# Moving the SBUF addresses of all split-product operands to one residue: 128 modulo 256 bytes

## The chip, the cores and the metric

The kernel is one program on one core of a Trainium2 chip. The metric is device time in microseconds (us), the median of several runs. A profile is one execution taken by the hardware profiler. Engines: TensorE (PE for matmuls, PEld for its weight loads), VectorE (DVE), ScalarE (ACT), GpSimd (POOL) and SyncE (SP, which here issues most DMAs).

## The reference

A sequence of 512 tokens with width 1024 runs through three blocks, all in float32:

```python
# block 1, layer 0: state-space mixer (SSD), then a convolutional FFN (width 2816)
# block 1, layer 1: conformer convolution (31 taps), then the same kind of FFN
h = h + mixer(rms_norm(h, norm_mix[i]))
h = h + (silu(gt) * val) @ down_w      # gt, val = split(causal_dwconv(rms_norm(h) @ up_w))
# block 2: hybrid mixer (latent attention + S5 scan + gates), memory cross attention,
x = layer_norm(ALPHA * x + mix); x = layer_norm(ALPHA * x + xattn(x, mem))
# then a mixture of 64 experts, top 8, expert width 256, plus a shared expert
x = layer_norm(ALPHA * x + moe(x))
```

## The kernel before

**Split products.** Most matrix products are made from three passes. An operand w is split into a high part (a copy of w rounded to the type fp32r, made by ScalarE) and a low part (w minus the high part, made by VectorE). The product is hi·hi + hi·lo + lo·hi, each pass a matmul with 512 moving columns of fp32r, accumulated in PSUM. I call three such matmuls a triple. In `proj_split` (the matmul is line 1289) it reads:

```python
for q, (wp, xp) in enumerate(((0, 0), (0, 1), (1, 0))):
    ins = nc.tensor.matmul(b[:], parts[wp][:, kk, m * P:(m + 1) * P], xparts[xp][:, kk, :],
                           start=n_k == 0 and q == 0, stop=n_k == k - 1 and q == 2)
```

The first operand is the stationary one (128 columns, loaded by LDWEIGHTS while the matmul before it streams), the second the moving one. The same triple stands in `project` (lines 1396 to 1398, the SSD input projection, four banks in turn), `proj_halves` (1313), `proj_abreast` (1337, the conformer's input projection, two banks in turn), the FFN's first slot (1545 to 1547), the conformer's taps (1590 to 1592, with diagonal weights and a moving operand that shifts by 4 bytes from tap to tap), the query projection (1815 to 1817), and the experts (1983 to 1985 gate and up, 2005 to 2007 down; there the tokens are stationary and the weights move). Other products, such as line 1245 and 1800, are plain float32 matmuls.

**Buffers.** Long-lived buffers are declared one after the other: `ident`, `ones`, `tri`, `stri`, `kc` (four constants), `pcol` (parameters as columns), `hT`, `uT`, `sq` (each 8 x 512 floats), two weight slots `wring`, four row buffers `raw` of 515 floats, `std`, `rinv`, and a large `arena`. The stages carve their own buffers out of the arena with `carve` and `carve_r`, by a running offset `top`. Each declaration is rounded up to 32 bytes. `ident` begins at byte 16512 of each partition, which is 128 modulo 256. The 16 bytes of `kc` (rounded to 32) shift all that follows, and the `raw` rows (2060 bytes, rounded to 2080) shift `std`, `rinv` and the arena.

**Where the operands begin**, modulo 256 bytes, worked out from the declarations (a slice of a weight or activation buffer begins at a multiple of 512 bytes inside it, so the residue of the buffer is that of its slices):

| operands | stage | before | after |
| --- | --- | --- | --- |
| `hT`, `uT`, `sq`, `wring` and their fp32r views | all | 160 | 128 |
| arena, whole multiples of 64 floats inside it (`yhi`, `ff_lo`, `gm`, `xe_hi`, `xe_lo`, `wdn`, `act_hi`) | several | 32 | 128 |
| `whi`, `ffhi`: high parts at the arena's end | FFN, mixers | 224 | 128 |
| `wgu_hi[0]`, `wdn_hi`: high parts of expert weights | experts | 180 | 128 |
| `dghi`, `dglo`: diagonal weights of taps | conformer | 224 | 128 |
| `hghi`, `hglo`: moving rows of taps | conformer | 224 and 88, plus 4 per tap | 128, plus 4 per tap |

So one triple's pairs of moving and stationary residues are: lines 1396 to 1398, all 160; L1289 on `sq_r`, `uT_r`, L1337 and L1313, moving 160, stationary 224 (high weights) and 160 (low weights); the FFN's down projection, moving 224 and 32, stationary 160; the SSD output projection, moving 32, stationary 224 and 160; the experts, moving 160 and 160 or 180 and 160, stationary 32 (down: moving 180 and 32, stationary 32).

**The order of work.** TensorE runs through the stages in program order: SSD (to about 340 us), its output projection (to 500), FFN 0 (to 860), conformer (to 1080), FFN 1 (to 1465), hybrid mixer and cross attention (to about 2080), experts (to about 2720), final sums. SP loads weight slots ahead, each when the matmuls that read the slot's last contents are done. In the experts' loop `m_step` SP loads 3 MB per expert into a ring of four, ScalarE and VectorE split them, and POOL gathers tokens and scatters results by indirect DMA.

Of the kernel before, what the change touches and what calls it, by code (L numbers as in the profile page):

```python
# [32 lines left out]
P = 128  # L33
T = 512
D = 1024
NK = D // P
TC = T // P
NSLOT = 2
NBANK = 4
SLOT = 8 * 512  # L40
PAD = 3
# [50 lines left out]
def cols(ap, i, n):  # L92

    return ap[:, i:i + n] if isinstance(i, int) else ap[:, bass.ds(i, n)]
# [55 lines left out]
def build(nc, A, out):  # L150

    ctx = ExitStack()
    with ctx:
        def sb(name, shape, dt=F32):
            return ctx.enter_context(nc.sbuf_tensor(name, shape, dt))

        def sb2(name, shape):

            with nc.sbuf_tensor(name + "_r", shape, F32R) as r:
                pass  # L160
            return sb(name, shape), r
# [27 lines left out]
        ones = sb("ones", [P, P])  # L189
        tri = sb("tri", [P, P])  # L190
        stri = sb("stri", [P, P])
        kc = sb("kc", [P, 4])
        pcol = sb("pcol", [P, NPB * P])
        hT, hT_r = sb2("hT", [P, NK, T])
        uT, uT_r = sb2("uT", [P, NK, T])
        sq, sq_r = sb2("sq", [P, NK, T])
        wring, wlo = zip(*[sb2(f"wring{r}", [P, SLOT]) for r in range(NSLOT)])
        raw = [sb(f"raw{r}", [P, PAD + T]) for r in range(NBANK)]
        std = sb("std", [P, T])
        rinv = sb("rinv", [P, T])  # L200
        ARENA = 28080
        arena, arena_r = sb2("arena", [P, ARENA])

        top = [0]

        def carve(*shape, dt=F32, at_=None):

            n = int(np.prod(shape))
            if dt == BF16:
                n = (n + 1) // 2  # L210
            a = top[0]
            top[0] += n
            assert top[0] <= ARENA, (top[0], ARENA)
            ap = arena[:, a:a + n]
            if dt != F32:
                ap = ap.bitcast(dt)
            if len(shape) == 2:
                ap = ap.rearrange("p (a b) -> p a b", b=shape[1])
            elif len(shape) == 3:
                ap = ap.rearrange("p (a b c) -> p a b c", b=shape[1], c=shape[2])  # L220
            return ap

        def carve_r(*shape):

            a = top[0]
            ap = carve(*shape)
            r = arena_r[:, a:top[0]]
            return ap, r if len(shape) == 1 else r.rearrange("p (a b) -> p a b", b=shape[1])

        def pcols(name, i, n=1):  # L230
            return cols(pcol, par.base[name] + i, n)
# [35 lines left out]


        pk = carve(NPB, P)
        xtok = carve(TC, D)  # L270

        top[0] = 0
# [29 lines left out]

        top[0] = ARENA - NSLOT * SLOT

# [15 lines left out]
        first_whi = carve_r(max(len(ks) for ks in FFN_EARLY), P)  # L320
        top[0] = ARENA - FFN_TILES * T
        ffhi = carve_r(FFN_TILES, T)
# [2 lines left out]

        top[0] = NBANK * T
        hg = carve(NK, T + CONF_TAPS - 1)
        glu_a = [carve(T) for _ in range(2)]
        glu_b = [carve(T) for _ in range(2)]
        cv = carve(NK, T)  # L330
        xc = sq
        HGW = T + CONF_TAPS - 1
        lnsq = arena[:, NBANK * T:NBANK * T + NK * T].rearrange("p (a b) -> p a b", b=T)
        top[0] += NK * T
        cvb = [carve(T) for _ in range(2)]
        hghi = [carve_r(HGW) for _ in range(2)]
        top[0] -= 2 * HGW + 2 * T + NK * T
        DIAGS = 10
        dghi, dglo = [list(d) for d in zip(*[(carve_r(P), carve_r(P)) for _ in range(DIAGS)])]
        hglo = [carve_r(HGW) for _ in range(2)]  # L340
        tapc_hi = carve_r(CONF_TAPS * NK)
        tapc_lo = carve(CONF_TAPS * NK)
        assert top[0] <= ARENA - NSLOT * SLOT
        PE_TAPS = [11] * (NK - 1) + [16]
# [10 lines left out]
        mag8 = carve(16, CHUNKS)  # L355
        sc_consts = carve(CONST_COLS)
        cos8 = carve(16, CHUNKS)
        GATE_TOP = 17924
        assert top[0] <= GATE_TOP
        top[0] = GATE_TOP  # L360
        posi = carve(T, dt=I32)
# [3 lines left out]
        wkr = carve(NK, 64)  # L365
        top[0] = ARENA - NSLOT * SLOT - 16 * CHUNKS
        sin8 = carve(16, CHUNKS)
# [84 lines left out]
        memk = carve(2, D)  # L452
        assert top[0] <= GATE_TOP
        top[0] -= 2 * D
        memc, mT_lo = carve_r(NK, 256)
        top[0] = GATE_TOP
        memq, mT_hi = carve_r(NK, 256)
# [46 lines left out]
        rsw = [carve(2) for _ in range(RING)]  # L504
        swt = [r[:, 1:2] for r in rsw]
        sidf = carve(1)
        slotrow = carve(P)
        slotcol = carve(2)
        posm = carve(TC, NE)
        rinfo = carve_r(TC * NE, 6)[1]  # L510
        cntf = carve(1)
        cnti = carve(1, dt=I32)
        moe_top = top[0]
        wgu_hi = (carve_r(SLOT)[1], flat(hT_r))
        wdn_hi = [carve_r(2 * D)[1] for _ in range(2)]
        top[0] = moe_top
# [3318 lines left out]
```

## Time and profile before

| | |
| --- | --- |
| median of 3 runs | 2789.91 us (2785.39 to 2795.55) |
| span of the profiled execution, first to last instruction | 2782.8 us |
| the profiled execution's own device time | not given beside its span |
| TensorE (PE) busy | 2680.2 us, 96% |
| weight loads (PEld) | 2057.9 us, 74% |
| VectorE, ScalarE, GpSimd busy | 72%, 50%, 9% |
| HBM | 165 GB/s over the span |

A matmul's busy time in the records (some 395 ns for 512 columns) overlaps that of the next one: its end is modelled. How fast matmuls follow each other is read from their starts in the timeline. A stretch in which PE is "busy" can therefore still contain slack of some nanoseconds for each matmul.

### The profile page before, as it was taken

What the parts mean: (1) busy time and instruction counts of PE and PEld (TensorE: products, weight loads), DVE (VectorE), ACT (ScalarE), POOL (GpSimd) and SP (SyncE); (2) the same over time, 40 slices, a digit from 0 to 9 for tenths busy, and PEclk for the clock granted to TensorE, in tenths of its full rate; (3) what the DMA queues carried; (4) which work ended last, traced back from release to release, by engine and by line L of the source; (5) the groups of instructions that cost most, each with busy time, mean ns of one, the idle gap of its engine ahead of it and who ended that gap; (6) DMA issues with size and microseconds to landing.
All of it is one profiled execution on the core that took longest, in us unless ns stands there. A gap on an engine that the chain in (4) does not pass through costs nothing.

```text
span 2782.8 us, 36214 instructions
## 1 busy us (share of the span) xinstructions
PE 2680.2 (96%) x12549; PEld 2057.9 (74%) x12549; DVE 1992.0 (72%) x3046; ACT 1397.4 (50%) x2137; POOL 240.5 (9%) x209
## 2 busy tenths in 40 slices
PE   8999999999999999999999989999899999999996
PEld 7877877788887877888876756676557777777772
DVE  4788744777727976778538546465559999999996
ACT  4767552222325545222324333444448887787782
POOL 0000000000000000000004400000013332212210
PEclk9999999999999999999999999999999999999998
DMA  3222212233232131233333561323449999999996
GB/s 112 72 61 68 91 61 95 88 101 103 69 104 91 61 35 61 91 103 99 83 95 122 135 124 54 107 70 120 161 173 359 358 359 361 359 352 352 349 340 255
DMA packets 258832, 435.11 MB, mean 156 GB/s; under 512 B 44315, under 2 KB 197987, under 8 KB 233891
## 3 DMA queue, kind: packets, MB, share of 16 engines
q1 hardware_dynamic: 240931, 395.61, 42.7%
q0 software_dynamic: 17792, 38.06, 4.5%
q8 instruction: 67, 1.10, 0.2%
q14 instruction: 42, 0.34, 0.0%
HBM read 416.33 MB, written 42.43 MB: 165 GB/s over the span
## 4 chain that ended last, share of the span: by engine, by line
PE 74%; DMA 12%; DVE 8%; ACT 3%; issue 2%; SPq 1%; DVEq 0%; ACTq 0%
PE tp L1289 40%; DMA wring<-in_w_exp_gu 10%; PE tp L1245 4%; PE tp L1983 2%; PE tp L1984 2%; PE tp L1985 2%; PE tp L1337 2%; PE tp L1396 2%; PE tp L1398 1%; PE tp L1397 1%; DVE wring_r L3676 1%; PE tp L1800 1%; DMA wring<-ytab 1%; PE mp L1591 1%; PE mp L1590 1%
## 5 line engine op out<-in xcount | busy, mean ns | idle before, releaser
L1289 PE MATMUL tp<-sq_r,arena_r 128*128 128x512 f32 x1056 | 417.1, 395 | 3.5 <-DVE uT_r L2820 3.5
L1289 PE MATMUL tp<-uT_r,arena_r 128*128 128x512 f32 x1056 | 417.9, 396 | 0.0
L1289 PE MATMUL tp<-sq_r,wring_r 128*128 128x512 f32 x1056 | 417.3, 395 | 0.0
L1289 PEld LDWEIGHTS tp<-sq_r,arena_r 128*128 128x128 f32 x1056 | 198.3, 188 | 55.9 <-issue 5.8
L1289 PEld LDWEIGHTS tp<-uT_r,arena_r 128*128 128x128 f32 x1056 | 198.3, 188 | 48.4 <-issue 1.4
L1289 PEld LDWEIGHTS tp<-sq_r,wring_r 128*128 128x128 f32 x1056 | 198.4, 188 | 44.0
L2792 DVE TENSOR_TENSOR wring_r<-wring,arena_r 128x2048 fp32r<-128x2048 f32 x82 | 187.1, 2322 | 56.6 <-ACT arena_r L2111 56.4
L1289 PE MATMUL tp<-arena_r,wring_r 128*128 128x512 f32 x564 | 223.7, 397 | 0.0
L2359 ACT ACTIVATE arena<-arena 128x512 f32<-128x512 f32 x44 | 27.8, 633 | 296.6 <-DVE arena L2878 296.5
L2111 ACT ACTIVATE arena_r<-wring 128x2048 fp32r<-128x2048 f32 x82 | 152.4, 1905 | 43.9 <-DMA wring<-in_b_pw_w 11.9
L3682 DVE TENSOR_TENSOR arena_r<-arena,arena_r 128x1024 fp32r<-128x1024 f32 x128 | 150.4, 1216 | 0.5 <-ACT arena_r L2705 0.5
L2878 DVE SCALAR_TENSOR_TENSOR arena<-raw,pcol,arena 128x512 f32<-128x512 f32 x176 | 132.3, 752 | 20.7 <-DVE arena L2878 4.9
L2098 ACT ACTIVATE raw<-tp 128x512 f32<-128x512 f32 x78 | 45.6, 599 | 200.7 <-PE tp L1289 133.9
L1168 POOL DMA_INDIRECT ytab<-arena x64 | 99.0, 1547 | 437.0 <-ACT arena L2724 430.7
L1289 PE MATMUL tp<-arena_r,sq_r 128*128 128x512 f32 x436 | 136.2, 393 | 0.0
L1289 PE MATMUL tp<-arena_r,uT_r 128*128 128x512 f32 x436 | 136.2, 393 | 0.0
L1396 PE MATMUL tp<-sq_r,wring_r 128*128 128x512 f32 x320 | 129.8, 406 | 0.9 <-DVE wring_r L2928 0.9
L2705 ACT ACTIVATE arena_r<-arena 128x1024 fp32r<-128x1024 f32 x128 | 127.8, 1051 | 0.0
L1398 PE MATMUL tp<-sq_r,wring_r 128*128 128x512 f32 x320 | 126.1, 394 | 0.0
L1397 PE MATMUL tp<-uT_r,wring_r 128*128 128x512 f32 x320 | 126.1, 394 | 0.0
L1289 PEld LDWEIGHTS tp<-arena_r,wring_r 128*128 128x128 f32 x564 | 105.7, 187 | 25.6
L2874 DVE TENSOR_TENSOR raw<-tp,rinv 128x512 f32<-128x512 f32 x88 | 60.5, 687 | 70.0 <-PE tp L1289 69.5
(582 smaller groups left out, 6209.2 us busy)
## 6 DMA issues: line engine op xcount, KB each, us to landing
arena<-in_w_exp_down SPq DMA_DIRECT2D x64, 1024.0 KB, 28.4
wring<-in_w_exp_gu SPq DMA_DIRECT2D x64, 1024.0 KB, 10.4
uT<-in_w_exp_gu SPq DMA_DIRECT2D x32, 1024.0 KB, 9.4
sq<-in_w_exp_gu SPq DMA_DIRECT2D x32, 1024.0 KB, 11.1
wring<-in_f_up_w SPq DMA_DIRECT2D x22, 1024.0 KB, 5.2
wring<-in_f_up_w SPq DMA_DIRECT2D x44, 512.0 KB, 6.6
wring<-in_f_down_w SPq DMA_DIRECT2D x32, 448.0 KB, 5.6
wring<-in_a_in_proj SPq DMA_DIRECT2D x42, 256.0 KB, 2.8
```

The lines of the kernel that those rows point to most:

```text
L1168: G.indirect_dma_start(out=ytab, out_offset=bass.IndirectOffsetOnAxis(ap=ridx[q][0:CAP, :], axis=0), in_=ye[b][0:CAP, :], in_offset=None, ...
L1245: ins = nc.tensor.matmul(b[lo:hi, 0:n], w, x, start=k == 0, stop=k == len(mms) - 1)
L1289: ins = nc.tensor.matmul(b[:], parts[wp][:, kk, m * P:(m + 1) * P], xparts[xp][:, kk, :], start=n_k == 0 and q == 0, stop=n_k == k - 1 and ...
L1396: nc.tensor.matmul(bank[:], w_hi[:, kk, cs], u_hi[1][:, kk, :], start=kk == 0, stop=False)
L1397: nc.tensor.matmul(bank[:], w_hi[:, kk, cs], u_lo[1][:, kk, :], start=False, stop=False)
L1398: ins = nc.tensor.matmul(bank[:], w_lo[:, kk, cs], u_hi[1][:, kk, :], start=False, stop=kk == NK - 1)
L2111: nc.scalar.activation(hi[r][1][:, a:b], wring[r][:, a:b], ACT.Copy).then_inc(whi_ready, 1)
L2705: nc.scalar.activation(wdn_hi[b][:, s], wdn[q][:, s], ACT.Copy).then_inc(moe["dhi"], 1)
L2792: V.tensor_tensor(wlo[r][:, a:b], wring[r][:, a:b], hi[r][1][:, a:b].bitcast(F32), ALU.subtract).then_inc(wlo_ready, 1)
L2874: V.tensor_tensor(r[:, PAD:PAD + T], tp[tiles.s % NBANK][:], rinv[:], ALU.mult).then_inc(tile_evac, 1)
L2878: ins = V.scalar_tensor_tensor(dst, r[:, PAD - t:PAD - t + T], w(taps - 1 - t), dst, ALU.mult, ALU.add)
L3682: V.tensor_tensor(wdn_lo[q][:, s], wdn[q][:, s], wdn_hi[b][:, s].bitcast(F32), ALU.subtract).then_inc(moe["dlo"], 1)
```

## The change

All operands of split products are given the residue 128 modulo 256 bytes. `kc` and the `raw` rows move into one tensor `tail` behind the arena, so that all large buffers follow `stri` without an odd size between. The arena grows by 16 floats. Odd sizes inside it are rounded up to 64 floats (`align`, `HGA`), and the experts' high parts are carved from the arena's end and no longer from `moe_top`. `slotrow` moves from the arena into a dead part of `pcol`. No instruction is added or taken away; four `raw` rows now begin at 2060-byte steps.

```diff
-        kc = sb("kc", [P, 4])
         pcol = sb("pcol", [P, NPB * P])
...
-        raw = [sb(f"raw{r}", [P, PAD + T]) for r in range(NBANK)]
         std = sb("std", [P, T])
         rinv = sb("rinv", [P, T])
-        ARENA = 28080
+        ARENA = 28096
         arena, arena_r = sb2("arena", [P, ARENA])
+        tail = sb("tail", [P, NBANK * (PAD + T) + 4])
+        raw = [tail[:, r * (PAD + T):(r + 1) * (PAD + T)] for r in range(NBANK)]
+        kc = tail[:, NBANK * (PAD + T):NBANK * (PAD + T) + 4]
...
+        LINE = 64
+
+        def align():
+
+            top[0] = -(-top[0] // LINE) * LINE
...
         hg = carve(NK, T + CONF_TAPS - 1)
+        align()
...
-        hghi = [carve_r(HGW) for _ in range(2)]
-        top[0] -= 2 * HGW + 2 * T + NK * T
+        HGA = -(-HGW // LINE) * LINE
+        hghi = [carve_r(HGA) for _ in range(2)]
+        top[0] -= 2 * HGA + 2 * T + NK * T
...
-        hglo = [carve_r(HGW) for _ in range(2)]
+        hglo = [carve_r(HGA) for _ in range(2)]
+        hghi, hglo = [[(f[:, 0:HGW], r[:, 0:HGW]) for f, r in h] for h in (hghi, hglo)]
...
-        GATE_TOP = 17924
+        GATE_TOP = 17920
...
-        slotrow = carve(P)
+        slotrow = pcols("a_conv_w", 0, P)
...
         moe_top = top[0]
+        assert moe_top <= ARENA - 2 * SLOT
+        top[0] = ARENA - 2 * SLOT
         wgu_hi = (carve_r(SLOT)[1], flat(hT_r))
         wdn_hi = [carve_r(2 * D)[1] for _ in range(2)]
         top[0] = moe_top
```

## Rows read from the trace of the kernel before

**Rows 1.** The page: busy time of each engine, and the chain that ended last.

```profile
PE 2680.2 (96%) x12549; PEld 2057.9 (74%) x12549; DVE 1992.0 (72%) x3046; ACT 1397.4 (50%) x2137; POOL 240.5 (9%) x209
...
PE 74%; DMA 12%; DVE 8%; ACT 3%; issue 2%; SPq 1%; DVEq 0%; ACTq 0%
```

**Rows 2.** Windows: stretch, length, busy (count) by engine, PEclk, DMA share, GB/s.

```profile
500.00:740.00 240.00, 240.00 (x1031) 193.02 (x1030) 186.75 (x231) 65.83 (x68) 0.00 (x0) 1.00 0.29 90
...
2300.00:2600.00 300.00, 288.09 (x1444) 223.76 (x1443) 283.42 (x432) 235.72 (x348) 65.88 (x58) 1.00 0.96 355
```

**Rows 3.** The page's costliest groups, four of split products: count, busy, mean.

```profile
L1289 PE MATMUL tp<-sq_r,arena_r 128*128 128x512 f32 x1056 | 417.1, 395 | 3.5 <-DVE uT_r L2820 3.5
...
L1289 PE MATMUL tp<-arena_r,wring_r 128*128 128x512 f32 x564 | 223.7, 397 | 0.0
...
L1289 PE MATMUL tp<-arena_r,sq_r 128*128 128x512 f32 x436 | 136.2, 393 | 0.0
...
L1398 PE MATMUL tp<-sq_r,wring_r 128*128 128x512 f32 x320 | 126.1, 394 | 0.0
```

**Rows 4.** Timeline, PE, SSD input projection: start, length, instruction; 13 matmuls between.

```profile
301.70 0.39 PE L1396 MATMUL tp<-sq_r,wring_r 128*128 128x512 f32 x1
...
304.88 0.39 PE L1398 MATMUL tp<-sq_r,wring_r 128*128 128x512 f32 x1
```

**Rows 5.** Timeline, PE, FFN 0 up and hybrid input projections; 23 matmuls between, each time.

```profile
560.04 0.40 PE L1289 MATMUL tp<-uT_r,arena_r 128*128 128x512 f32 x1
...
565.64 0.40 PE L1289 MATMUL tp<-uT_r,arena_r 128*128 128x512 f32 x1
...
1605.27 0.40 PE L1289 MATMUL tp<-sq_r,arena_r 128*128 128x512 f32 x1
...
1610.87 0.40 PE L1289 MATMUL tp<-sq_r,arena_r 128*128 128x512 f32 x1
```

**Rows 6.** Timeline, PE, conformer input projection; 47 matmuls between.

```profile
867.58 0.39 PE L1337 MATMUL tp<-sq_r,arena_r 128*128 128x512 f32 x1
...
878.67 0.39 PE L1337 MATMUL tp<-sq_r,arena_r 128*128 128x512 f32 x1
```

**Rows 7.** Timeline, PE, FFN 0 down projection; 26 matmuls between.

```profile
799.76 0.40 PE L1289 MATMUL tp<-arena_r,wring_r 128*128 128x512 f32 x1
...
806.00 0.40 PE L1289 MATMUL tp<-arena_r,wring_r 128*128 128x512 f32 x1
```

**Rows 8.** Timeline, PE, conformer taps: a whole triple from each of two channels.

```profile
888.38 0.39 PE L1590 MATMUL mp<-arena_r 128*128 128x512 f32 x1
...
889.07 0.40 PE L1590 MATMUL mp<-arena_r 128*128 128x512 f32 x1
...
914.23 0.40 PE L1590 MATMUL mp<-arena_r 128*128 128x512 f32 x1
...
914.93 0.40 PE L1289 MATMUL tp<-sq_r,arena_r 128*128 128x512 f32 x1
```

**Rows 9.** Timeline, PE, one expert: 17, then 11 matmuls between.

```profile
2400.76 0.39 PE L1983 MATMUL tp<-hT_r,arena_r 128*112 128x512 f32 x1
...
2404.93 0.40 PE L2005 MATMUL mp<-arena_r 128*112 128x512 f32 x1
...
2407.75 0.93 PE L1972 MATMUL tp<-ident,arena 112*128 112x112 f32 x8
```

**Rows 10.** The chain in order of time: a plain float32 product, start and length.

```profile
1905.41 13.73 PE tp L1800 x32
```

**Rows 11.** Waits, 2300 to 2600 us: who waited for whom, us, times, longest.

```profile
ACT arena_r L2698 <- DMA uT<-in_w_exp_gu: 17.2, 8, 2.4
...
PE mp L1993 <- DVE std L3688: 11.8, 27, 0.9
```

**Rows 12.** Two lines' own instructions: duration min/median/max in ns.

```profile
L2878 DVE SCALAR_TENSOR_TENSOR arena<-raw,pcol,arena x176: 750/752/755, 495.1 to 1339.1; 128x512 f32<-128x512 f32 x176
...
L3676 DVE TENSOR_TENSOR uT_r<-uT,arena_r x64: 1212/1219/1226, 2065.8 to 2679.9; 128x1024 fp32r<-128x1024 f32 x64
```

## The prediction

> **What bounds the kernel now.** I read the page first. TensorE is busy for 96% of the span and holds 74% of the chain that ended last; DMA holds 12%, VectorE 8% [rows 1]. The windows say where that holds. In FFN 0's up projection PE is busy for all 240 us at the full granted clock (1.00), VectorE for 187 us and the DMA engines for a share of 0.29: only TensorE can set the pace there. In the experts' loop three things are near their limit at once: PE 288 of 300 us, VectorE 283 us, and a DMA share of 0.96 at 355 GB/s [rows 2].
>
> "Busy" is not the whole story, because a matmul's record (395 ns) reaches over the next one. I therefore read the starts in the timeline, over stretches without a gap, and divide. This is the view on which the prediction rests:
>
> - SSD input projection, all residues 160: 301.70 to 304.88 us for 14 matmuls, 227.1 ns each [rows 4].
> - FFN 0 up, moving 160, stationary 224 and 160: 5.60 us for 24, 233.3 ns; hybrid input projection, the same residues: 5.60 us for 24, 233.3 ns [rows 5].
> - Conformer input projection, the same residues: 11.09 us for 48, 231.0 ns [rows 6].
> - FFN 0 down, moving 224 and 32, stationary 160: 6.24 us for 27, 231.1 ns [rows 7].
> - One expert, moving 160, stationary 32: 4.17 us for 18, 231.7 ns; its down product, moving 180 and 32, stationary 32: 2.82 us for 12, 235.0 ns [rows 9].
>
> The stage in which moving and stationary operands share a residue is the fastest by 4 to 8 ns a matmul. The order of the loops is a poor explanation: the conformer's projection also changes banks from triple to triple, runs the same three passes from the same `sq_r` and `uT_r`, and takes 231.0 ns, not 227.1. What differs beside the place of the high weights (residue 224 against 160) is hard to find. Residues alone do not fix the number, though: FFN 0 and the conformer have the same ones and differ by 2.3 ns. A plain float32 product is no witness: L1800 takes 13.73 us for 32 records, 429 ns each [rows 10], which is close to twice 512 columns at 2.4 GHz, and here moving and stationary lie at 160 too.
>
> **The change part by part.** It adds and removes no instruction. Its terms are these.
>
> 1. Triples before the experts, outside SSD and taps. The groups give 3 x 1056 + 564 + 2 x 436 = 4604 matmuls [rows 3] (the other two of the 1056 and the other 436 are the remaining passes of the same triples); by the program's loops the other split products of 512 columns are 772. Together 5376. Of these FFN 0's window holds 1031 [rows 2], and the hybrid input projection is six slots of 96, so 576: some 1,600 at 233.3 ns. The other 3,776 I take at 231.0. If all come to 227.1, the first lose 6.2 ns each, 9.9 us, and the rest 3.9 ns, 14.7 us. Sum 24.6 us. PE's weight loads do not stand in the way: PEld is busy 193 of 240 us in FFN 0 [rows 2]. VectorE has 53 us free in that window, some 22%, and the stage shrinks by 2.7%, so nothing new becomes late.
> 2. SSD's 3 x 320 matmuls [rows 3] have equal residues already; they keep them. Zero.
> 3. The conformer's taps, 279 matmuls. The moving operand shifts by 4 bytes from tap to tap, so it cannot keep a residue. Two triples read 0.69 us (moving 224) and 0.70 us (moving 128, stationary 224) [rows 8]. They range within about 5 ns of what they have, both ways, which is 1.4 us for 279. I take zero.
> 4. The experts: 64 times 36 matmuls, 2304. At 227.1 an expert would save 18 x 4.6 (24 x 4.6 for the whole gate and up product) and 12 x 7.9 ns, thus 110 + 95 = 0.2 us, 13 us in all. But the DMA engines are full there, and ScalarE waits for an expert's weights, 17.2 us in 8 waits for one of four such buffers, while PE waits 11.8 us in 27 short ones [rows 11]. A faster PE hands SP its buffers earlier, and the load only queues longer. Bounds: 0 and 13 us. I take 1, since DMA sets the pace and only the start of the loop and small holes in the share of 0.96 can give anything.
> 5. The S5 and attention parts run between short dependences. Some of term 1's matmuls there may be hidden; I take 1 us off.
> 6. `raw` rows now begin at 2060-byte steps, so their starts differ modulo 16. The convolution L2878 already reads `raw` shifted by one and two floats: all 176 take 750 to 755 ns. And L3676 reads `uT` at residue 160 and the high part at 180 in 1212 to 1226 ns [rows 12]. VectorE does not notice. Zero. `slotrow` in `pcol` is written once and read as before: zero; even 1% on VectorE's work in the experts, some 6 us, is hidden while DMA leads, and would be the bound if that cover went.
> 7. The weights' DMA destinations move from 160 or 32 to 128 modulo 256, multiples of 32 bytes before and after; four loads and four stores on `raw` rows at the end of the program are no longer so. The window's 355 GB/s [rows 2] comes from a mix of both old residues. Zero, with 0.3% of the experts' 600 us, 2 us, as its bound either way.
>
> Sum: 24.6 + 1 - 1 = about 25 us. The profiled execution spans 2782.8 us, 7 us under the median of 2789.9; its own device time is not given, so I take the difference from the median: **2765 us**.
>
> The Trainium skill speaks against this change. "SBUF — State Buffer", section "Who interferes with whom", gives TensorE two read ports, one for the moving operand and one for weight loads, independent of each other and of every engine. By that rule residues could not matter and the sum would be zero instead of 25 us. The trace has 227.1 against 231.0 and 233.3 ns [rows 4 to 6], which the rule leaves without a cause.
>
> **The rivals.**
>
> *No change.* The interval depends on something that goes with the SSD stage and not on residues: that it takes its two weight parts from the two `wring` slots rather than from the arena, or other engines' traffic. For: FFN 0 and the conformer differ at equal residues [rows 5, 6]. Against: the down projection has all its weights in `sq` and `wring`, stationary residue 160, and still takes 231.1 [rows 7]. Time 2790. It is what the skill's rule on the ports would give.
>
> *The experts give too.* If TensorE, busy 288 of 300 us, is the pacemaker and the DMA share of 0.96 has room, term 4 pays 13 us: 2753.
>
> *Aligned starts give more.* Every big buffer now begins on a multiple of 64 bytes; the old residues 160, 224 and 32 are all 32 modulo 64. The triples of the trace are 681 (3 x 227.1), 693 and 700 ns: they lie on steps of about 6.7 ns. If a start on a multiple saves one more step for each matmul, 5376 + 960 of them give 42 us more: 2765 - 42 = 2723. Against: the tap at moving residue 128 shows no such saving, 0.70 us a triple [rows 8]. "TensorE: Matmul & The Clock Gate", section "Wait — 56ns, not 53.3ns?" of the Trainium skill, has 215.7 ns between starts at 512 bf16 columns on a warm array; no row of this kernel comes near it.
>
> *A slower residue.* Equal residues alone are not enough: the tap whose moving and stationary operands lie at 224 takes 0.69 us a triple, 230 ns a matmul, and the only triple with a moving operand at 128 takes 0.70 us, 233.3 ns [rows 8]. Should 128 itself be a poor residue, all triples go to 234: SSD's 960 lose 6.9 ns each (6.6 us), the 1,600 lose 0.7 (1.1 us), the 3,776 lose 3.0 (11.3 us): +19 us, 2809. It decides the sign where the new mean passes about 231 ns over the 6,336 matmuls.
>
> **How the numbers follow.** Equal residues at 227, only before the experts: 0.47, with a range of its own of 2758 to 2773. No change: 0.18. Experts give too: 0.10. Aligned starts give more: 0.10. Slower residue: 0.15. What a measurement of this kernel can tell from no change is 0.3%, 8.4 us. Faster by more than that: 0.47 + 0.10 + 0.10 = 0.67; same 0.18; slower 0.15. The range leaves out the far side of the aligned case and most of the slower one: 2743 to 2797.
>
> **What would show it.** In the changed profile, 24 matmuls of FFN 0's up projection should span 5.45 us, not 5.60; the conformer's 48 should span 10.9; SSD's 14 stay at 3.18. The experts' loop should start some 24 us earlier and last as long as before, at 355 to 360 GB/s. L2878 stays at 752 ns. The prediction is wrong if intervals at 128 differ from those that SSD has at 160, or if the experts' loop changes its length by more than 3 us.

## The result, and the profile after

| | before | after |
| --- | --- | --- |
| median, 4 runs each on one chip | 2788.90 us (2785.39 to 2795.55) | 2753.56 us (2752.41 to 2756.62) |
| ratio, with its 95% interval | | 0.9879 (0.9864 to 0.9894) |
| span of the profiled execution | 2782.8 us | 2750.7 us |
| device time of that execution | not given | 2752.41 us |

The changed kernel takes 30 to 38 us less, 35 by the medians. Lines after the declarations have moved down by 12: L1289 is now L1301, L1337 is L1349, L1396 to 1398 are L1408 to 1410, L1983 and L2005 are L1995 and L2017, L2878 and L3676 are L2890 and L3688.

The page of the changed kernel, its span, its busy times and its chain, answers to [rows 1]:

```profile
span 2750.7 us, 36214 instructions
...
PE 2646.7 (96%) x12549; PEld 2054.1 (75%) x12549; DVE 1989.9 (72%) x3046; ACT 1398.5 (51%) x2137; POOL 232.0 (8%) x209
...
PE 72%; DMA 10%; DVE 10%; issue 3%; ACT 3%; DVEq 0%; SPq 0%; ACTq 0%
```

TensorE's share of the span is 96% before and after, and it still holds most of the chain. To see what became faster, read the starts again. Timeline of TensorE in the changed kernel, columns as in [rows 4]; SSD, FFN 0 up, FFN 0 down, conformer:

```profile
300.06 0.39 PE L1408 MATMUL tp<-sq_r,wring_r 128*128 128x512 f32 x1
...
303.23 0.39 PE L1410 MATMUL tp<-sq_r,wring_r 128*128 128x512 f32 x1
...
559.87 0.39 PE L1301 MATMUL tp<-sq_r,arena_r 128*128 128x512 f32 x1
...
565.31 0.39 PE L1301 MATMUL tp<-sq_r,arena_r 128*128 128x512 f32 x1
...
790.17 0.39 PE L1301 MATMUL tp<-arena_r,wring_r 128*128 128x512 f32 x1
...
796.29 0.39 PE L1301 MATMUL tp<-arena_r,wring_r 128*128 128x512 f32 x1
...
856.91 0.39 PE L1349 MATMUL tp<-sq_r,arena_r 128*128 128x512 f32 x1
...
867.79 0.39 PE L1349 MATMUL tp<-sq_r,arena_r 128*128 128x512 f32 x1
```

- SSD: 14 matmuls in 3.17 us, 226.4 ns (two rounded ends); before 3.18 [rows 4]. It had equal residues already, and did not change. (Its 226.4 and the 227.1 of before are the same interval: two ends rounded to 10 ns are worth 0.7 ns over 14 matmuls.)
- FFN 0 up: 24 in 5.44 us, 226.7 ns; before 5.60, 233.3 [rows 5].
- FFN 0 down: 27 in 6.12 us, 226.7 ns; before 6.24, 231.1 [rows 7].
- Conformer: 48 in 10.88 us, 226.7 ns; before 11.09, 231.0 [rows 6].

A record's own length (0.39 us) hardly moves, so busy time alone would not have shown where the gain is. The starts do.

The experts, same view: the last gate and up matmuls of one expert, its down product, and the transposes behind it.

```profile
2401.31 0.39 PE L1995 MATMUL tp<-arena_r 128*112 128x512 f32 x1
...
2406.21 0.39 PE L2017 MATMUL mp<-arena_r 128*112 128x512 f32 x1
...
2409.00 0.45 PE L1984 MATMUL tp<-ident,arena 112*128 112x112 f32 x3
```

21 matmuls in 4.90 us are 233.3 ns, and 12 in 2.79 us are 232.5; before 231.7 and 235.0 [rows 9]. Here equal residues brought little. Two windows, columns as in [rows 2]:

```profile
500.00:735.00 235.00, 235.00 (x1038) 194.58 (x1037) 188.57 (x235) 66.27 (x68) 0.00 (x0) 1.00 0.30 93
...
2300.00:2600.00 300.00, 285.46 (x1449) 223.67 (x1448) 284.49 (x432) 236.71 (x348) 65.84 (x59) 1.00 0.96 355
```

FFN 0 puts 1038 matmuls into 235 us where 1031 took 240 [rows 2], at the same clock of 1.00. The experts have the same DMA share and GB/s as before. Their loop, from the first gate and up matmul to the last (one line's instructions, first and last start):

```profile
L1995 PE MATMUL tp<-arena_r x256: 388/394/737, 2037.5 to 2676.0; 128*112 128x512 f32 x128
L1995 PE MATMUL tp<-hT_r,arena_r x256: 388/394/749, 2048.4 to 2684.6; 128*112 128x512 f32 x128
```

And the same view of the kernel before:

```profile
L1983 PE MATMUL tp<-arena_r x256: 396/398/748, 2067.6 to 2707.5; 128*112 128x512 f32 x128
L1983 PE MATMUL tp<-hT_r,arena_r x256: 388/394/489, 2077.9 to 2716.0; 128*112 128x512 f32 x128
```

The loop starts at 2037.5 instead of 2067.6 us, 30.1 earlier, and takes 647.1 instead of 648.4 us. So 30.1 of the 32.1 us of the span were gained ahead of the experts, 1.3 in them and 0.7 behind them. The waits in the experts show who sets their pace; they answer to [rows 11]:

```profile
ACT hT_r L2710 <- DMA wring<-in_w_exp_gu: 17.2, 8, 2.4
ACT arena_r L2710 <- DMA uT<-in_w_exp_gu: 16.3, 7, 2.8
...
PE mp L2005 <- DVE std L3700: 14.5, 27, 1.2
```

ScalarE still waits for the experts' weights from DMA. The chain of the changed kernel agrees for the middle of the loop: between 2300 and 2400 us a DMA of expert weights holds 85 of the 100 us, as before. Between 2100 and 2200 us it runs through TensorE and VectorE instead. One piece of it, start and length:

```profile
2303.66 28.97 DMA wring<-in_w_exp_gu
```

TensorE, now slightly ahead, waits 14.5 us for VectorE in 27 short waits; it was 11.8 [rows 11]. The two VectorE lines did not notice the move; they answer to [rows 12]:

```profile
L2890 DVE SCALAR_TENSOR_TENSOR arena<-tail,pcol,arena x176: 750/752/755, 491.0 to 1318.6; 128x512 f32<-128x512 f32 x176
...
L3688 DVE TENSOR_TENSOR uT_r<-uT,arena_r x64: 1212/1218/1226, 2036.2 to 2648.8; 128x1024 fp32r<-128x1024 f32 x64
```

For a number that a few rows can't give, I took the mean over all start-to-start intervals without a hole (up to 260 ns) in each stage, from the same trace. In ns, before and after: SSD 227.8 and 227.7; SSD output 231.4 and 227.3; FFN 0 up 233.2 and 226.7, down 231.1 and 226.7; conformer with its taps 232.2 and 229.6 (the taps alone 233.9 and 233.4); FFN 1 up 231.1 and 226.7, down 231.2 and 226.7; hybrid input 232.5 and 227.4, the rest of that block 232.0 and 227.0; experts' gate and up 233.4 and 230.7, down 234.0 and 230.5. Such means are called stage means below.

Most stage means have a simple make-up. The time from one triple to the next is 680 ns in nearly every triple of the changed kernel's FFNs. In most stages with unequal residues its average is 680 ns and one, two or three steps of some 6.7 ns: 687, 693 or 700 ns, which are 228.9, 231.1 and 233.3 ns a matmul. (Not in all: e7's FFN 0 up has 231.8 ns and e4's FFN 0 down 232.4.) FFN 0 up went from 700 to 680 ns and FFN 1 up from 693 to 680. SSD's triples take 680 ns too, before and after, except the first few behind a break of its stretches, which take 684 to 697 ns. That is why its mean is 227.7 and not 226.7.

### The profile page after: what moved, and what is told of

It reads as the page before. It is cut to its first block, busy times and chain, and to the rows that moved or that the text cites. A ratio compares the mean times of both kernels' runs of the same rounds, so it can differ in the third digit from the quotient of the medians.

```text
span 2750.7 us, 36214 instructions
## 1 busy us (share of the span) xinstructions
PE 2646.7 (96%) x12549; PEld 2054.1 (75%) x12549; DVE 1989.9 (72%) x3046; ACT 1398.5 (51%) x2137; POOL 232.0 (8%) x209
## 4 chain that ended last, share of the span: by engine, by line
PE 72%; DMA 10%; DVE 10%; issue 3%; ACT 3%; DVEq 0%; SPq 0%; ACTq 0%
PE tp L1301 40%; DMA wring<-in_w_exp_gu 9%; PE tp L1257 4%; PE tp L1408 2%; DVE wring_r L3688 2%; PE tp L1410 2%; PE tp L1409 2%; PE tp L1349 2%; PE tp L1995 2%; PE tp L1997 2%; PE tp L1996 2%; PE tp L1812 1%; DMA wring<-ytab 1%; PE mp L1603 1%; PE mp L1604 1%
## 5 line engine op out<-in xcount | busy, mean ns | idle before, releaser
L1301 PE MATMUL tp<-sq_r,arena_r 128*128 128x512 f32 x1056 | 415.3, 393 | 3.5 <-DVE uT_r L2832 3.5
L1301 PE MATMUL tp<-sq_r,wring_r 128*128 128x512 f32 x1056 | 411.4, 390 | 0.0
L1301 PE MATMUL tp<-uT_r,arena_r 128*128 128x512 f32 x1056 | 411.2, 389 | 0.0
L1301 PEld LDWEIGHTS tp<-sq_r,arena_r 128*128 128x128 f32 x1056 | 198.5, 188 | 48.8 <-issue 5.8
L1301 PEld LDWEIGHTS tp<-uT_r,arena_r 128*128 128x128 f32 x1056 | 198.5, 188 | 42.3 <-issue 1.4
L1301 PEld LDWEIGHTS tp<-sq_r,wring_r 128*128 128x128 f32 x1056 | 198.3, 188 | 41.8
L1301 PE MATMUL tp<-arena_r,wring_r 128*128 128x512 f32 x564 | 219.4, 389 | 0.0
L2890 DVE SCALAR_TENSOR_TENSOR arena<-tail,pcol,arena 128x512 f32<-128x512 f32 x176 | 132.3, 752 | 20.7 <-DVE arena L2890 4.9
L2110 ACT ACTIVATE tail<-tp 128x512 f32<-128x512 f32 x78 | 45.6, 601 | 193.8 <-PE tp L1301 129.6
L1301 PE MATMUL tp<-arena_r,sq_r 128*128 128x512 f32 x436 | 134.6, 390 | 0.0
L1301 PE MATMUL tp<-arena_r,uT_r 128*128 128x512 f32 x436 | 134.5, 389 | 0.0
L1408 PE MATMUL tp<-sq_r,wring_r 128*128 128x512 f32 x320 | 129.6, 405 | 0.9 <-DVE wring_r L2940 0.9
L1180 POOL DMA_INDIRECT ytab<-arena x64 | 90.2, 1409 | 445.4 <-ACT arena L2736 438.5
L1301 PEld LDWEIGHTS tp<-arena_r,wring_r 128*128 128x128 f32 x564 | 105.9, 188 | 21.9
L1995 PE MATMUL tp<-hT_r,arena_r 128*112 128x512 f32 x256 | 104.5, 408 | 0.0
```

The costliest lines, as they stand in the source:

```text
L1180: G.indirect_dma_start(out=ytab, out_offset=bass.IndirectOffsetOnAxis(ap=ridx[q][0:CAP, :], axis=0), in_=ye[b][0:CAP, :], in_offset=None, ...
L1408: nc.tensor.matmul(bank[:], w_hi[:, kk, cs], u_hi[1][:, kk, :], start=kk == 0, stop=False)
L1995: nc.tensor.matmul(tp[b][0:CAP, :], x_hi, hi[:, k, :], start=k == 0, stop=False)
L2890: ins = V.scalar_tensor_tensor(dst, r[:, PAD - t:PAD - t + T], w(taps - 1 - t), dst, ALU.mult, ALU.add)
```

## The experiments

All edits are made to the changed kernel, and every ratio is to the kernel before on the same chip. Three theories were at issue. **Equality**: a matmul is fast when its moving operand and the stationary operand loaded beside it begin at the same residue modulo 256 bytes. **Value**: the residue 128 is good by itself, or multiples of 64. **Side**: what counts is which buffers moved (the arena and its contents), not how they stand to the others. Equality is what the prediction rests on.

### Same residue, other values: e1 and e2

In e1 everything from `pcol` on lies at 160, in e2 at 0.

```diff
 # e1_all160
+        pad = sb("pad", [P, 8])
         pcol = sb("pcol", [P, NPB * P])
 # e2_all0: the tail block first, then 16 floats, and nothing else between
+        tail = sb("tail", [P, NBANK * (PAD + T) + 4])
+        pad = sb("pad", [P, 16])
         pcol = sb("pcol", [P, NPB * P])
...
-        ARENA = 28096
+        ARENA = 28032
```

> The changed kernel with 32 bytes of padding ahead of pcol, so that every operand of a split product lies at 160 modulo 256 and no longer at 128. If only the equality of the residues counts, a matmul in every stage before the experts follows the last one after 227 ns, as at 128, and the time is that of the changed kernel, 2754 us within 4. If the residue 128 itself is the good one (a multiple of 64 bytes), the intervals go back to 231 to 233 ns outside the SSD stage, and the time to 2780 or more.

> The changed kernel with the raw rows and 64 bytes of padding ahead of pcol (and an arena shorter by 64 floats, which nothing uses): every operand at 0 modulo 256. If only equality counts: 227 ns and 2754 us within 4. If starts on a 256-byte boundary save one more step of 6.7 ns for each of some 6300 matmuls: 220 ns and 2712 us. If residue 0 is a poor one: 231 ns or more, 2775 us or more.

e1: 2755.55 us, ratio 0.9872 (0.9856 to 0.9889). e2: 2752.69 us, ratio 0.9867 (0.9849 to 0.9884). In both, FFN 0 up takes 5.44 us for 24 matmuls. Timeline of TensorE in e1:

```profile
559.66 0.39 PE L1302 MATMUL tp<-sq_r,arena_r 128*128 128x512 f32 x1
...
565.10 0.39 PE L1302 MATMUL tp<-sq_r,arena_r 128*128 128x512 f32 x1
```

The value 128 does nothing by itself. 160 is not a multiple of 64 and is as fast, so alignment is not it either.

### The arena alone moved away: e3, e4, e7 and e10

These take the equality away again, by four distances: the arena at +64, +128, +32 and +16 bytes against `hT`, `uT`, `sq` and `wring`, which stay at 128. In an up projection's triple that makes two pairs unequal; the third, with the low weights in `wring`, stays equal.

```diff
 # e3_arena64: tail moved from behind the arena to ahead of it
+        tail = sb("tail", [P, NBANK * (PAD + T) + 4])
         arena, arena_r = sb2("arena", [P, ARENA])
 # e4_arena128: the same, and 16 floats more
+        pad = sb("pad", [P, 16])
 # e7_arena32: tail stays behind, 8 floats ahead of the arena
+        pad = sb("pad", [P, 8])
         arena, arena_r = sb2("arena", [P, ARENA])
 # e10_arena16
-        arena, arena_r = sb2("arena", [P, ARENA])
+        whole, whole_r = sb2("arena", [P, ARENA + 4])
+        arena, arena_r = whole[:, 4:4 + ARENA], whole_r[:, 4:4 + ARENA]
```

> The changed kernel with the raw rows between rinv and arena: uT, sq, wring at 128, everything in the arena at 192, a difference of 64 bytes as the high weights had before. If the difference between operands of one triple is the cause: the up projections back at 231 to 233 ns, the down projections at 231, and the time at about 2780 us; the taps and the experts partly keep their gain, since inside the arena all is still equal. If the old loss came from something else (odd sizes, the place of kc, the expert parts at 180), the time stays at 2754 us.

> The same with 64 bytes more: uT, sq, wring at 128, the arena at 0, a difference of 128 bytes. If the residues count modulo 256: 231 ns or more outside the SSD stage and about 2775 to 2785 us. If they count modulo 128 only: 227 ns and 2754 us.

> The changed kernel with 32 bytes of padding ahead of the arena: uT, sq, wring at 128, the arena at 160. If any difference modulo 256 costs, as 64 and 128 bytes do: 231 to 233 ns outside SSD and 2775 to 2785 us. If only a difference of 64 bytes or more does: 227 ns and 2754 us.

> The changed kernel with the arena shifted by 16 bytes: uT, sq, wring at 128, the arena at 144. If any difference modulo 256 costs, as 32, 64 and 128 bytes do: 231 to 233 ns outside SSD and 2775 to 2786 us. If differences below 32 bytes are free: 227 ns and 2754 us.

| run | arena against the others | median, us | ratio (95%) | 24 matmuls of FFN 0 up | of FFN 1 up | stage mean, SSD |
| --- | --- | --- | --- | --- | --- | --- |
| e10 | +16 | 2775.18 | 0.9965 (0.9951 to 0.9979) | 5.60 us | 5.50 us | 227.8 ns |
| e7 | +32 | 2785.11 | 0.9985 (0.9974 to 0.9996) | 5.57 | 5.57 | 227.8 |
| e3 | +64 | 2779.38 | 0.9963 (0.9948 to 0.9978) | 5.54 | 5.60 | 227.7 |
| e4 | +128 | 2785.53 | 0.9984 (0.9972 to 0.9996) | 5.60 | 5.60 | 227.8 |

Timeline of TensorE in e10, FFN 0 up:

```profile
559.78 0.40 PE L1302 MATMUL tp<-sq_r,arena_r 128*128 128x512 f32 x1
...
565.38 0.40 PE L1302 MATMUL tp<-sq_r,arena_r 128*128 128x512 f32 x1
```

A shift of the arena alone takes back 69 to 88% of the gain (from 0.9879 to 0.9963 and 0.9985), at any distance tried; 16 bytes bring FFN 0 up fully back to 5.60 us. SSD, whose triples do not touch the arena, stays where it was. Which of the values between 229 and 233 ns a stage takes does not follow from the distance: at +64 FFN 0 is faster than FFN 1, at +16 slower, with the same residues in both. The 229 ns of FFN 1 up in e10 (and of its down projection in e3, below) lie under the 231 to 233 that I had expected.

### The other side moved: e5 and e6

In e5 `hT`, `uT` and `sq` stay at 128, and `wring` and the arena go to 192. This makes SSD's pairs unequal and the SSD output projection's equal. In e6 only `hT` and `uT` stay at 128: of each triple of the FFN's up projection one matmul (the one moving `uT_r`) is unequal and two are equal.

```diff
 # e5_weights64: the tail block between sq and wring
         sq, sq_r = sb2("sq", [P, NK, T])
+        tail = sb("tail", [P, NBANK * (PAD + T) + 4])
         wring, wlo = zip(*[sb2(f"wring{r}", [P, SLOT]) for r in range(NSLOT)])
 # e6_uT64: the tail block between uT and sq
         uT, uT_r = sb2("uT", [P, NK, T])
+        tail = sb("tail", [P, NBANK * (PAD + T) + 4])
         sq, sq_r = sb2("sq", [P, NK, T])
```

> The changed kernel with the raw rows between sq and wring: hT, uT, sq at 128, wring and the arena at 192. In the SSD and the up projections the moving operands then all lie at 128 and the stationary ones all at 192; nothing changes its residue from one matmul to the next on either side. If what costs is a difference between the moving operand and the stationary one being loaded beside it: 231 ns or more in both stages, also in SSD, where every kernel so far has 227.8, and 2780 us or more. If what costs is the change of residue from one matmul to the next on the same side: 227 ns in these stages, and only the down projections (high weights in uT and sq at 128, low ones in wring at 192) slow, some 2760 us.

> The changed kernel with the raw rows between uT and sq: hT and uT at 128, sq, wring and the arena at 192. In the SSD and the up projections only the moving low part lies apart, one matmul in three. By the difference theory that one matmul in three costs some 7 ns more or both its neighbours do: a mean of 229 to 231 ns in SSD and up projections, 2765 to 2785 us. By the theory of a change on the same side the moving side changes twice in each triple: 231 ns. If moving operands do not matter and only the stationary ones do: 227 ns.

e5: 2784.74 us, ratio 0.9984 (0.9975 to 0.9994). Timeline of TensorE in e5, SSD and FFN 0 up:

```profile
302.07 0.39 PE L1409 MATMUL tp<-uT_r,wring_r 128*128 128x512 f32 x1
...
305.34 0.39 PE L1408 MATMUL tp<-sq_r,wring_r 128*128 128x512 f32 x1
...
559.68 0.40 PE L1301 MATMUL tp<-sq_r,wring_r 128*128 128x512 f32 x1
...
565.28 0.40 PE L1301 MATMUL tp<-sq_r,wring_r 128*128 128x512 f32 x1
```

SSD's 14 matmuls now take 3.27 us, 233.6 ns (stage mean 233.2; 227.7 in the changed kernel). It is the only run in which all three matmuls of SSD's triples are unequal, and the only one with SSD near 233; in e6 below one in three is unequal there, and the mean is 229.4. The part of the SSD output projection that is equal at 192 (its moving operands in the arena) has 226.8 ns. The side theory has it the other way round in both places, so it falls. So does the theory named in the expectation, that a change of residue from one matmul to the next on the same side costs: in e5 SSD's moving operands all lie at 128 and its stationary ones all at 192, and it is slow. So does the rival that ties the speed to the stage or to the two `wring` slots: same stage, same slots, 5.5 ns slower.

The section "Who interferes with whom" of the Trainium skill's page "SBUF — State Buffer" gives TensorE's moving port and its weight port no influence on each other. By it e5 would equal the changed kernel in SSD; the measurement decides against it, 233.2 against 227.7 ns.

e6: 2767.94 us, ratio 0.9921 (0.9905 to 0.9938). Timeline of TensorE in e6:

```profile
559.71 0.39 PE L1301 MATMUL tp<-sq_r,wring_r 128*128 128x512 f32 x1
...
565.20 0.39 PE L1301 MATMUL tp<-sq_r,wring_r 128*128 128x512 f32 x1
```

5.49 us for 24 are 228.8 ns, one step of 6.7 ns for each triple, which has one unequal pair; SSD in e5, with three unequal pairs, lost three steps. That looks like a price per pair, but other stages of the same runs do not keep to it. The FFN's down projection has its high weights in `uT` and `sq` by turns. In e6 the tiles with `sq` (all pairs equal) take 680 ns a triple and those with `uT` (two pairs unequal) 687, tile by tile in turn: equality decides within one stage. Two unequal pairs cost one step there, and in e5's FFN 0 down as well. In e3 all three pairs of both down projections are unequal by 64 bytes, and the two FFNs differ. Timeline of TensorE in e3, ten triples of FFN 0 down, then ten of FFN 1 down:

```profile
790.65 0.40 PE L1301 MATMUL tp<-arena_r,wring_r 128*128 128x512 f32 x1
...
797.65 0.40 PE L1301 MATMUL tp<-arena_r,wring_r 128*128 128x512 f32 x1
...
1352.85 0.39 PE L1301 MATMUL tp<-arena_r,wring_r 128*128 128x512 f32 x1
...
1359.72 0.39 PE L1301 MATMUL tp<-arena_r,wring_r 128*128 128x512 f32 x1
```

700 and 687 ns a triple. Together, all at a distance of 64 bytes:

| run and stage | unequal pairs of three | ns a triple, mean |
| --- | --- | --- |
| e6, FFN 0 down, high weights in `sq` | 0 | 680 |
| e6, FFN 0 up | 1 | 687 |
| e6, FFN 0 down, high weights in `uT` | 2 | 687 |
| e5, FFN 0 down | 2 | 687 |
| before, FFN 0 up and FFN 1 up | 2 | 700 and 693 |
| e5, SSD | 3 | 700 |
| e3, FFN 0 down and FFN 1 down | 3 | 700 and 687 |

Before the experts, equal pairs gave 680 ns in every stretch without breaks, and in this table every stage with an unequal pair lost one to three steps. The number of steps does not follow from the number of unequal pairs. Nor do these runs tell which stationary operand counts for a moving one, its own or the one loaded for the next matmul: in all the stages quoted either the moving or the stationary operands of a triple share one residue, so both readings count the same number of unequal pairs.

### The experts: e8 and e9

Why did the experts gain so little, in their matmuls and in time? e8 puts the high parts of the experts' weights back at residue 20 and leaves all else. e9 gives the stationary operand, the tokens of an expert, 128 columns instead of 112, with larger gathers and scatters.

```diff
 # e8_moe_top
-        assert moe_top <= ARENA - 2 * SLOT
-        top[0] = ARENA - 2 * SLOT
 # e9_cap128
-        NE, CAP, NTOK, RING, TOPK = 64, 112, T, 8, 8
+        NE, CAP, NTOK, RING, TOPK = 64, 128, T, 8, 8
```

> The changed kernel with the experts' high parts carved from moe_top again, where they lie at 20 modulo 256, and all else at 128. The experts' matmuls go from 230.6 ns back to some 234, 2304 x 3.4 = 8 us more TensorE work. If DMA sets the pace there, as I said: the experts' loop keeps its 652 us within 3, and the time stays at 2754 within 4. If TensorE does: 2762 us.

> The changed kernel with 128 token places per expert and no longer 112, so that a stationary operand in the experts is a whole 512 bytes, as everywhere else, and not 448. It explains why the experts' matmuls stay at 230.6 ns with equal residues, where all other stages have 226.7. If the width of the stationary operand is the cause: 227 ns. If the traffic of DMA, VectorE and ScalarE in that loop is: still 230 to 231 ns. The loop itself stays at some 652 us by the reading that DMA sets its pace, or grows a little with the larger gathers.

e8: 2757.42 us, ratio 0.9883 (0.9867 to 0.9900), which can't be told from the full change's 0.9879. Its experts' stage means rise to 232.5 and 234.9 ns, from 230.7 and 230.5, and the loop takes 645.5 us, not 647.1. One line's instructions in e8:

```profile
L1993 PE MATMUL tp<-arena_r x256: 395/402/747, 2043.4 to 2679.9; 128*112 128x512 f32 x128
L1993 PE MATMUL tp<-hT_r,arena_r x256: 388/394/485, 2053.8 to 2688.9; 128*112 128x512 f32 x128
```

So the part of the change that aligned the experts' high weights gives faster matmuls and no time.

e9: 2760.27 us, ratio 0.9909 (0.9889 to 0.9928). Timeline and window of e9:

```profile
2401.01 0.39 PE L2017 MATMUL mp<-arena_r 128*128 128x512 f32 x1
...
2403.74 0.38 PE L1984 MATMUL tp<-ident,arena 128*128 128x128 f32 x2
...
2300.00:2600.00 300.00, 287.73 (x1457) 241.83 (x1456) 289.16 (x437) 241.62 (x347) 80.58 (x58) 1.00 0.93 355
```

12 matmuls in 2.73 us, 227.5 ns; stage means 227.9 and 226.7. With 128 columns the experts reach what the other stages have. Whether it is the width of the weight load or the 128 output rows, this run does not tell. The loop takes 648.9 us, longer if anything, at the same 355 GB/s. (The expectations have 652 us for the loop by another count of its ends; here it is always the first and the last start of one line.)

Over all kernels run, the experts' loop took 641 to 649 us in the profiled executions, while the experts' stage means went from 227 to 235 ns, and the one does not follow the other: 648.9 us in e9 with the fastest matmuls, 645.5 in e8 with nearly the slowest, 648.4 before. The shortest, 641.0 us in e4, has the highest rate in the window from 2300 to 2600 us, 360 GB/s. One window of e4:

```profile
2300.00:2600.00 300.00, 290.77 (x1475) 227.33 (x1474) 288.34 (x440) 240.48 (x354) 72.24 (x59) 1.00 0.97 360
```

That this comes from the arena's place is not shown by one execution, and it was not followed up.

e8 and e9 show that the pace of TensorE's matmuls does not set the loop's length; e8 is the clean one, since e9 also makes the gathers and scatters larger. That DMA sets it, rather than VectorE, which is busy for 284 of 300 us, rests on the chain and on the DMA share of 0.96. No run changed DMA or VectorE alone.

## Why the prediction was right

The forecast of 2765 us fell 11 us above the median, inside the range, on the side named, by the mechanism named. By its steps:

1. **Triples before the experts, 24.6 us.** Right in cause (e3, e4, e7 and e10 take most of it away; e1 and e2 keep it) and slightly low in size. The common value is 226.7 ns and not 227.1: the stretch of SSD that I read has it too, and the 0.4 ns are the rounding of its two ends. With the stage means FFN 0 up gives 1,031 x 6.5 = 6.7 us, the hybrid input 576 x 5.1 = 2.9, and the other 3,769 some 4.3 ns each, 16.2: about 26 us. The profile shows 30.1, but the start of the experts' loop scatters: 2037.5, 2042.4, 2039.9, 2043.4 and 2043.0 us in the changed kernel, e1, e2, e8 and e9, which do not differ in their pairs before it. Their mean is 26.4 us ahead of the kernel before's 2067.6, and there is one profile of that.
2. **SSD, zero.** Right: 3.17 us for 14, and the stage mean 227.7 against 227.8.
3. **Taps, zero.** Right: their moving residue changes from tap to tap, so nearly all their pairs stay unequal, and their own mean went from 233.9 to 233.4 ns, 0.1 us for 279.
4. **Experts, 1 us of at most 13.** Right in time, 1.3 us, and the reason given holds so far that faster or slower matmuls do not move the loop (e8, e9). What I had not seen: the matmuls themselves did not reach 227 with 112 columns, so even the upper bound of 13 us assumed too much, 230.6 ns being about half the way.
5. **S5 and attention, -1 us.** Not needed. The rest of the hybrid block went from 232.0 to 227.0 ns, and its 384 matmuls became 2.0 us shorter, which is all of it. The hybrid input projection's 2.9 us show as 0.9 here and as 2.5 in e2; the difference is a fall of the clock (below) and not hidden work.
6. **VectorE, zero.** Right: 752 ns and 1218 ns, both unchanged.
7. **DMA destinations, zero.** Right: 355 GB/s both times.

**Where the 30.1 us lie.** The starts of the same matmuls in both profiles say it. The stages of term 1 gave 24.1 us: the SSD output projection 2.4, FFN 0 9.4, the conformer 2.4, FFN 1 7.0, the hybrid input projection 0.9, and the 384 matmuls of triples between 1780 and 1876 us 2.0. The other 6 us lie in stretches of other work: 1.8 in SSD, 2.4 between 1625 and 1780 us (S5 and attention), and 1.8 between 1919 and 2011 us. SSD scatters: with its pairs unchanged it is from 0.4 us longer to 3.0 shorter than before in e1 to e4 and e7 to e10. The last two, and the small gain of the hybrid input projection, go with the granted clock. Windows of the kernel before, then one of the changed kernel, columns as in [rows 2]:

```profile
1735.10:1738.50 3.40, 3.40 (x13) 2.54 (x12) 1.62 (x7) 1.50 (x6) 0.00 (x0) 0.50 0.61 239
1745.30:1748.70 3.40, 3.40 (x17) 3.07 (x17) 0.00 (x0) 0.60 (x1) 0.00 (x0) 0.50 0.22 48
1956.90:1960.30 3.40, 3.40 (x13) 2.85 (x12) 0.00 (x0) 0.38 (x1) 0.00 (x0) 0.51 0.02 5
...
1487.60:1491.00 3.40, 3.40 (x12) 3.08 (x13) 3.40 (x3) 1.97 (x5) 3.32 (x2) 0.50 0.13 38
```

The clock fell to its lower level, 1.2 GHz, for 3.4 us at each of these places. The changed kernel's profile has none of the first three, and the kernel before has nothing like the fourth. In e2, whose profile has the two early falls and not the fourth, S5 and attention gained 0.6 us and the hybrid input projection 2.5. So the falls come at other places in programs whose pairs before the experts are the same, and the fourth cost some 1.6 us. No term of mine had them.

The forecast was right in the part it named: 24.6 us against 24.1 in this pair of profiles, or 25.7 without the fall at 1487.6 us. The rest of the way from 25 to the median difference of 35 us does not come from its terms: 6 us in stretches of other work, 1 more in and behind the experts than forecast, 1 that term 5 took off without need, and 3 because the profiled execution before lies 6 us below the median of its runs and the one after 3 below. That all of this lies on one side is chance. The difference itself is known only to between 30 and 38.

**The rivals.** *No change*: fell with the result, and e5 shows why, SSD in the same slots at 233 ns. *The experts give too*: fell; the loop kept its length within 1.3 us, and e8 and e9 show that slower or faster matmuls there do not move it. *Aligned starts give more*: fell; 0 and 128 give the 226.7 ns of 160, and no stage came nearer to the 215.7 ns of the Trainium skill's page "TensorE: Matmul & The Clock Gate" ("Wait — 56ns, not 53.3ns?"). *A slower residue*: fell; 128 has the same 226.7 ns as 160 and 0. The two taps of [rows 8] that fed this rival were poor evidence: two ends rounded to 10 ns, over three matmuls.

No version among these beats the change: e1 and e2 equal it within their intervals. A version with the experts' matmuls at 227 and the smaller gathers was not found.

## What to carry to other kernels

Read the starts of matmuls over a stretch without a hole and divide, and compare stages of the same shape: 226.7 against 231 to 233 ns is 2 to 3% that no busy share shows. If stages differ and their operands are fp32r, work out where the moving and the stationary operand begin in the partition, modulo 256 bytes; making all such buffers equal costs some padding and an order of declarations, and one small odd buffer among them undoes it. Then ask in which stages TensorE sets the pace: in the experts, where it did not, faster matmuls gave no time.

## What the runs showed of the hardware that I had not expected

- A split product's matmul of 512 fp32r columns starts every 226.7 ns if both operands begin at the same residue modulo 256 bytes (0, 128 and 160 were run), and loses 2 to 7 ns on the average if some of its triple's pairs do not. A difference of 16 bytes is enough (5.60 us for 24 in e10). A difference of 256 costs nothing: in the changed kernel the FFN's high weights begin at 384 modulo 512 bytes and the tokens at 128, and 226.7 ns is what they take.
- What an unequal pair costs is not fixed by the residues. The same pairs took 233.2 ns in FFN 0 and 231.1 in FFN 1 before; at +64 it was the other way round, 231.2 and 233.3, and the down projections took 233.3 and 228.9. A triple takes 680, 687, 693 or 700 ns in these stages. What chooses the value stays open.
- With 112 stationary columns equal residues gave 230.6 ns, with 128 columns 227.
- Plain float32 products with 512 columns do not show it. Line 1245 of the kernel before (1257 or 1258 in the others), with the moving operand in the arena and the stationary one in `uT` starts every 429.2 ns at residues 32 and 160 (before), 128 and 128 (the changed kernel), 0 and 128 (e4), and 144 and 128 (e10).
- In the SSD, S5 and attention stages the granted clock fell to 0.5 for 3.4 or 6.8 us, at places that partly differ from run to run though the instructions are the same. 3.4 us of it cost some 1.6 us in the hybrid input projection.
